# The weight tiles of a two-layer decoder kernel at the other end of SBUF

## The chip, the cores and the metric

The kernel runs on 1 core of one Trainium2 chip. The metric is the device time of one execution in microseconds (us), and the figure to be predicted is the median of several runs. Engines are named as the profile names them: PE (matrix multiplication), PEld (PE's weight loads), DVE, ACT, POOL, and SP, which only issues DMAs here.

## The reference

One sequence of 512 tokens with 1024 channels passes two layers. Four mixers (compressed and windowed attention, a diagonal state-space scan, a gated delta rule, a stick-breaking attention) work on slices of one large projection; their outputs are gated, projected and added, and a SwiGLU block follows.

```python
for l in range(DEPTH):                                   # 2
    h = rms_norm(x, attn_norm[l])
    proj = h @ w_in[l]                                   # 1024 x 6804
    (nsa_q, nsa_kv, nsa_g, s5_u, gdn_qkv, gdn_a, gdn_b, gdn_z, sb_qkv,
     merge_logits) = jnp.split(proj, IN_OFFSETS, axis=-1)
    o_nsa, o_s5, o_gdn, o_sb = ...                       # each (1, 512, 256)
    gates = jax.nn.sigmoid(merge_logits).reshape(B_, S_, N_BRANCH, D_MODEL)
    merged = jnp.zeros_like(x)
    for m, o_m in enumerate((o_nsa, o_s5, o_gdn, o_sb)):
        merged = merged + gates[:, :, m] * (o_m @ w_branch[l, m])
    x = x + merged @ w_out[l]
    x = x + swiglu_ffn(rms_norm(x, ffn_norm[l]), w_gate[l], w_up[l], w_down[l])   # 1024 -> 2816 -> 1024
```

## The kernel before, in words

Activations lie with the channels on the 128 partitions and the 512 tokens along the row. The weights stream through in slabs of 128 columns (512 KB, 4096 bytes a partition), 140 in each of the two layers, in one order that is written out by hand (`NAMES`). A slab passes three stations. SP's queue loads it into one of two places of `raw` (L426 and L430). ACT copies it into one of three places of `wH` with rounding to float32r (L1013). The rest, `raw - wH`, goes into `wL`, by POOL up to the first slabs of the branch projection (L1878) and by DVE from there on (L1331); that instruction also hands the place of `raw` back to SP.

Every large product is then made of three float32r matmuls, in the helper `mm3`: `wH x high`, `wH x low`, `wL x high`, where high and low are the two parts of the activation. They stand on L464, L465 and L466 of the kernel. The weights are the stationary operand (128 x 128, loaded by a LDWEIGHTS ahead of each matmul) and the activation is the moving operand (128 x 512). Which tiles move depends on the stage:

- the input projection, spread as `fill` between the small steps of the mixers, and the gate and up projections of the SwiGLU: `hH` and `hL`
- the branch projections: `oH` and `oL`, both in `arena`
- the output projection: `mH` and `mLow`, both in `pj`
- the down projection: `hidH` in `arena` and `hidL` from `pj` onward
- one pair of slabs a layer (`values`, "sbv") has the roles exchanged: `hH` and `hL` are loaded as weights and `wH` and `wL` move, 256 columns at a time.

SBUF is laid out by hand. The helper `sb` gives each tile the next free byte of the row, rounded up to 32 bytes, in the order of the calls; a tile with `at=` lies over another. Nothing else in the program depends on where a tile is.

Of the kernel before, what the change touches and what calls it, by code (L numbers as in the profile page):

```python
# [21 lines left out]
F32R = mybir.dt.float32r  # L22

P = 128
D = 1024
KT = D // P
# [73 lines left out]
RING = 2  # L100
SPLIT = 3
# [55 lines left out]
def program(nc, a_x, a_pos, a_const, a_pack, a_w, a_gates, a_out):  # L157
    with ExitStack() as ctx:
# [13 lines left out]
        def sb(name, shape, dt=F32, at=None, skip=0):  # L172

            size = int(np.prod(shape[1:])) * (2 if dt == BF16 else 4)
            if at is None:
                place[name] = top[0] = -(-top[0] // 32) * 32
                top[0] += size
            else:
                place[name] = place[at] + skip
            return nc.alloc_sbuf_tensor_at(name, shape, dt, offset=place[name])  # L180
# [4 lines left out]
        hH = sb("hH", [P, KT, S], F32R)  # L185
        hL = sb("hL", [P, KT, S], F32R)
        gload = sb("gload", [P, 4, 4, S], at="hH")
        raw = sb("raw", [P, RING, KT, P])
        wH = sb("wH", [P, SPLIT, KT, P], F32R)
        wL = sb("wL", [P, SPLIT, KT, P], F32R)  # L190
        cosT = sb("cosT", [P, S])
        sinT = sb("sinT", [P, S])
        small = sb("small", [P, 632])
# [9 lines left out]
        pj = sb("pj", [P, NPJ, S])  # L203
        sbv = sb("sbv", [P, NT, 256])
        gst = sb("gst", [P, 2, S])
        oH = sb("oH", [P, 8, S], F32R, at="arena")
        oL = sb("oL", [P, 8, S], F32R, at="arena", skip=4 * 4096)
        mH = sb("mH", [P, KT, S], F32R, at="pj")
# [1919 lines left out]
```

## Time and profile before

| | us |
|---|---|
| median of 3 runs | 2216.49 (2214.96 to 2217.32) |
| the profiled execution | 2215.63 |
| span of its instructions | 2213.8 |
| PE busy | 2059.3, 93% |
| DVE busy | 1196.2, 54% |
| ACT busy | 759.8, 34% |
| POOL busy | 540.4, 24% |

Busy means that an instruction of the engine was under way. PE's matmuls overlap in the records, so a busy PE says that it did not stand still, and not how fast it went; how fast is read from the distance of one matmul's start to the next one's.

### The profile page before, as it was taken

What the parts mean: (1) busy time and instruction counts of PE and PEld (TensorE: products, weight loads), DVE (VectorE), ACT (ScalarE), POOL (GpSimd) and SP (SyncE); (2) the same over time, 40 slices, a digit from 0 to 9 for tenths busy, and PEclk for the clock granted to TensorE, in tenths of its full rate; (3) what the DMA queues carried; (4) which work ended last, traced back from release to release, by engine and by line L of the source; (5) the groups of instructions that cost most, each with busy time, mean ns of one, the idle gap of its engine ahead of it and who ended that gap; (6) DMA issues with size and microseconds to landing.
All of it is one profiled execution on the core that took longest, in us unless ns stands there. A gap on an engine that the chain in (4) does not pass through costs nothing. (4 is left out here: it accounts for less than half of the span.)

```text
span 2213.8 us, 25834 instructions
## 1 busy us (share of the span) xinstructions
PE 2059.3 (93%) x10096; PEld 1651.2 (75%) x10096; DVE 1196.2 (54%) x1657; ACT 759.8 (34%) x1149; POOL 540.4 (24%) x304
## 2 busy tenths in 40 slices
PE   5998988899999999999979989889999999999998
PEld 3778977667777888888747879666577778888886
DVE  6635569764447555542266264796633575555421
ACT  5442231264335422222154422313642343322221
POOL 2435028523116000000034340484131240000000
PEclk9999989999989999999989999999999899999999
DMA  5221011222134233223242210113121442222332
GB/s 216 91 91 49 15 53 58 90 68 72 58 114 171 85 99 101 96 95 105 67 171 86 77 48 20 55 65 100 58 72 48 149 141 91 100 95 95 105 97 94
DMA packets 55124, 196.98 MB, mean 89 GB/s; under 512 B 6112, under 2 KB 6112, under 8 KB 52576
## 3 DMA queue, kind: packets, MB, share of 16 engines
q1 hardware_dynamic: 41184, 153.41, 21.1%
q10 hardware_dynamic: 13824, 41.95, 4.9%
q8 instruction: 82, 1.34, 0.3%
q14 instruction: 34, 0.28, 0.0%
HBM read 176.46 MB, written 18.87 MB: 88 GB/s over the span
## 5 line engine op out<-in xcount | busy, mean ns | idle before, releaser
L464 PE MATMUL bank<-hH,wH 128*128 128x512 f32 (+1 forms) x1536 | 617.5, 402 | 30.4 <-POOL wL L1878 14.9
L465 PE MATMUL bank<-hL,wH 128*128 128x512 f32 (+1 forms) x1536 | 605.7, 394 | 0.0
L466 PE MATMUL bank<-hH,wL 128*128 128x512 f32 (+1 forms) x1536 | 605.3, 394 | 0.0
L1878 POOL TENSOR_TENSOR wL<-raw,wH 128x1024 fp32r<-128x1024 f32 x114 | 282.2, 2480 | 1156.8 <-ACT wH L1013 1156.6
L1013 ACT ACTIVATE wH<-raw 128x1024 fp32r<-128x1024 f32 x276 | 289.6, 1051 | 295.8 <-PE bank L466 234.8
L464 PEld LDWEIGHTS bank<-hH,wH 128*128 128x128 f32 (+1 forms) x1536 | 291.9, 190 | 109.7 <-issue 30.1
L1331 DVE TENSOR_TENSOR wL<-raw,wH 128x1024 fp32r<-128x1024 f32 x162 | 214.2, 1322 | 253.0 <-ACT wH L1013 253.0
L466 PEld LDWEIGHTS bank<-hH,wL 128*128 128x128 f32 (+1 forms) x1536 | 291.0, 189 | 65.0 <-issue 1.1
L465 PEld LDWEIGHTS bank<-hL,wH 128*128 128x128 f32 (+1 forms) x1536 | 291.5, 190 | 62.1 <-issue 2.1
L1016 ACT ACTIVATE gst<-bank 128x512 f32<-128x512 f32 x64 | 38.2, 597 | 351.3 <-PE bank L466 351.3
L466 PE MATMUL bank<-hidH,wL 128*128 128x512 f32 x352 | 140.4, 399 | 0.0
L465 PE MATMUL bank<-hidL,wH 128*128 128x512 f32 x352 | 138.7, 394 | 0.0
L464 PE MATMUL bank<-hidH,wH 128*128 128x512 f32 x352 | 138.0, 392 | 0.0
L1647 DVE TENSOR_TENSOR arena<-arena 128x512 f32<-128x512 f32 x64 | 104.9, 1697 | 0.5
L1308 ACT ACTIVATE hidH<-arena 128x512 fp32r<-128x512 f32 x44 | 27.8, 633 | 191.3 <-DVE arena L1855 191.3
L1967 POOL TENSOR_TENSOR arena<-arena 128x512 f32<-128x512 f32 x48 | 80.8, 1685 | 25.3 <-DVE arena L1815 21.4
L1773 DVE TENSOR_REDUCE small<-bank 128x1 f32<-128x128 f32 (+3 forms) x64 | 30.8, 490 | 103.2 <-PE bank L876 101.8
L465 PEld LDWEIGHTS bank<-hidL,wH 128*128 128x128 f32 x352 | 66.1, 188 | 17.3
L464 PEld LDWEIGHTS bank<-hidH,wH 128*128 128x128 f32 x352 | 66.1, 188 | 15.7
L466 PEld LDWEIGHTS bank<-hidH,wL 128*128 128x128 f32 x352 | 66.1, 188 | 15.1
L1305 ACT ACTIVATE comp<-comp 128x512 f32<-128x512 f32 x44 | 27.8, 632 | 127.7 <-DVE comp L1846 127.7
L1642 DVE TENSOR_TENSOR_SCAN arena<-small,arena 128x512 f32<-128x512 f32 x32 | 58.1, 1855 | 0.5 <-POOL arena L1935 0.5
(394 smaller groups left out, 2988.0 us busy)
## 6 DMA issues: line engine op xcount, KB each, us to landing
raw<-weights SPq DMA_DIRECT2D x280, 512.0 KB, 3.5
gates<-gst ACTq DMA_DIRECT2D x64, 256.0 KB, 2.4
gload<-gates ACTq DMA_DIRECT2D x16, 1024.0 KB, 7.5
arena<-weights ACTq DMA_DIRECT2D x10, 512.0 KB, 9.0
xT<-x SPq DMA_DIRECT2D x1, 2048.0 KB, 9.8
pj<-weights ACTq DMA_DIRECT2D x4, 512.0 KB, 4.0
out<-xT SPq DMA_DIRECT2D x1, 2048.0 KB, 6.3
const<-constants SPq DMA_DIRECT2D x1, 1180.5 KB, 5.2
```

The source lines that it names most:

```text
L464: mm(out, a[0], b[0], start=start, stop=False)
L465: mm(out, a[0], b[1], start=False, stop=False)
L466: return mm(out, a[1], b[0], start=False, stop=stop)
L1013: act(wH[:, ORD[i] % SPLIT], raw[:, i % RING], ACT.Copy).then_inc(q["w_high"], 1)
L1016: act(out, stream(name)[:, :], ACT.Copy, scale=scale).then_inc(q["proj_taken"], 1)
L1305: act(ft[:, f % 2, :], fa[:, f % 2, :], ACT.Tanh, scale=0.5).then_inc(q["fg_tanh"], 1)
L1331: tt_(wL[:, ORD[i] % SPLIT], raw[:, i % RING], wH[:, ORD[i] % SPLIT].bitcast(F32), SU)\
L1642: v.tensor_tensor_scan(s5_z(i, j), mg, s5_m(i, 2 * j), 0.0, M, A_).then_inc(q["z_ready"], 1)
L1647: tt_(chunks(s5_m(i, j)), x, z, M).then_inc(q["n_ready"], 1)
L1773: v.tensor_reduce(nm[:, 4 * m + h:4 * m + h + 1], PS[2 + h % 2][:, 0:P * (m // 2 + 1)], AX_X, ALU.max, negate=True).then_inc(q["nm_ready"], 1)
L1878: tt_(wL[:, ORD[i] % SPLIT], raw[:, i % RING], wH[:, ORD[i] % SPLIT].bitcast(F32), SU)\
L1967: ins = tt_(mtmp[:, dt % 2, 0, :], mtmp[:, dt % 2, 0, :], mtmp[:, dt % 2, m, :], A_)
```

## The change: the place of three tiles

The three tiles `raw`, `wH` and `wL` (32,768 bytes a partition together) are given out last and no longer after `gload`. All that came behind them moves down by 32,768 bytes.

```diff
         hH = sb("hH", [P, KT, S], F32R)
         hL = sb("hL", [P, KT, S], F32R)
         gload = sb("gload", [P, 4, 4, S], at="hH")
-        raw = sb("raw", [P, RING, KT, P])
-        wH = sb("wH", [P, SPLIT, KT, P], F32R)
-        wL = sb("wL", [P, SPLIT, KT, P], F32R)
         cosT = sb("cosT", [P, S])
         sinT = sb("sinT", [P, S])
         small = sb("small", [P, 632])
...
         pj = sb("pj", [P, NPJ, S])
         sbv = sb("sbv", [P, NT, 256])
         gst = sb("gst", [P, 2, S])
+        raw = sb("raw", [P, RING, KT, P])
+        wH = sb("wH", [P, SPLIT, KT, P], F32R)
+        wL = sb("wL", [P, SPLIT, KT, P], F32R)
         oH = sb("oH", [P, 8, S], F32R, at="arena")
         oL = sb("oL", [P, 8, S], F32R, at="arena", skip=4 * 4096)
```

No instruction is added, removed or reordered on any engine, and no wait differs: the two programs are the same row by row but for the addresses in their operands. These are the starts that `sb` gives out, in bytes of a partition's row counted from the start of the first tile, `const`, which itself begins at a multiple of 128 (byte 16,512):

| tile | start before | remainder by 128, by 512 | start after | remainder by 128, by 512 |
|---|---|---|---|---|
| `hH` | 29,472 | 32, 288 | 29,472 | 32, 288 |
| `hL` | 45,856 | 32, 288 | 45,856 | 32, 288 |
| `raw` | 62,240 | 32, 288 | 179,584 | 0, 384 |
| `wH` | 70,432 | 32, 288 | 187,776 | 0, 384 |
| `wL` | 82,720 | 32, 288 | 200,064 | 0, 384 |
| `arena` (`oH`, `oL`, `hidH`) | 109,952 | 0, 384 | 77,184 | 0, 384 |
| `pj` (`mH`, `mLow`, `hidL`) | 167,296 | 0, 384 | 134,528 | 0, 384 |
| `gst` | 208,256 | 0, 384 | 175,488 | 0, 384 |

A place of a slab is 4096 bytes long and one k-step of a moving tile 2048, so the remainders hold for each of their pieces.

## Rows read from the trace of the kernel before

**Rows 1.** The page's head: busy us of each engine, share of the span, instructions.

```profile
PE 2059.3 (93%) x10096; PEld 1651.2 (75%) x10096; DVE 1196.2 (54%) x1657; ACT 759.8 (34%) x1149; POOL 540.4 (24%) x304
```

**Rows 2.** Stretches of layer 1: length, busy of PE, PEld, DVE, ACT, POOL, clock, DMA.

```profile
45.00:650.00 605.00, 554.94 (x3017) 444.21 (x3017) 346.87 (x510) 215.58 (x378) 221.88 (x123) 0.95 0.19 65
742.00:982.00 240.00, 240.00 (x1058) 198.33 (x1057) 128.95 (x156) 74.13 (x93) 0.00 (x0) 1.00 0.29 95
982.00:1110.00 128.00, 123.70 (x531) 99.18 (x529) 33.93 (x33) 23.82 (x23) 0.00 (x0) 1.00 0.27 87
```

**Rows 3.** PE's groups by shape, and one of its loads: count, busy us, mean ns, idle before.

```profile
L464 PE MATMUL bank<-hH,wH 128*128 128x512 f32 x1520 | 610.3, 401 | 20.4 <-POOL wL L1878 14.9 <-ACT arena L1085 5.5
L464 PE MATMUL bank<-hidH,wH 128*128 128x512 f32 x352 | 138.0, 392 | 0.0
L464 PE MATMUL bank<-oH,wH 128*128 128x512 f32 x128 | 52.3, 408 | 0.0
L464 PE MATMUL bank<-mH,wH 128*128 128x512 f32 x128 | 50.9, 398 | 2.7 <-DVE mLow L1335 2.7
L464 PE MATMUL bank<-wH,hH 128*128 128x256 f32 x64 | 18.9, 295 | 0.0
L464 PEld LDWEIGHTS bank<-hH,wH 128*128 128x128 f32 (+1 forms) x1536 | 291.9, 190 | 109.7 <-issue 30.1
```

**Rows 4.** Timeline of PE in the gate and up projections: start us, duration us.

```profile
900.04 0.39 PE L464 MATMUL bank<-hH,wH 128*128 128x512 f32 x1
...
902.08 0.39 PE L464 MATMUL bank<-hH,wH 128*128 128x512 f32 x1
```

**Rows 5.** The same in the down projection and, behind it, the output projection.

```profile
1029.94 0.39 PE L464 MATMUL bank<-hidH,wH 128*128 128x512 f32 x1
1030.17 0.39 PE L465 MATMUL bank<-hidL,wH 128*128 128x512 f32 x1
1030.40 0.40 PE L466 MATMUL bank<-hidH,wL 128*128 128x512 f32 x1
...
1032.04 0.39 PE L464 MATMUL bank<-hidH,wH 128*128 128x512 f32 x1
...
735.01 0.39 PE L464 MATMUL bank<-mH,wH 128*128 128x512 f32 x1
737.11 0.39 PE L464 MATMUL bank<-mH,wH 128*128 128x512 f32 x1
```

**Rows 6.** PE alone in three stretches: gate and up, down, branch projections.

```profile
755.00:980.00 225.00, 225.00 (x994) 1.00 0.31 99
985.00:1095.00 110.00, 110.00 (x473) 1.00 0.30 96
655.00:695.00 40.00, 40.00 (x173) 1.00 0.68 254
```

**Rows 7.** Timeline of PE where a projection slab starts after other work.

```profile
98.90 0.39 PE L465 MATMUL bank<-hL,wH 128*128 128x512 f32 x1
...
100.51 0.39 PE L466 MATMUL bank<-hH,wL 128*128 128x512 f32 x1
...
101.42 0.39 PE L464 MATMUL bank<-hH,wH 128*128 128x512 f32 x1
```

**Rows 8.** One line's instructions, ns min/median/max: ACT's rounding, DVE's and POOL's remainder.

```profile
L1013 ACT ACTIVATE wH<-raw x276: 1040/1049/1065, 19.0 to 2189.5; 128x1024 fp32r<-128x1024 f32 x138
L1331 DVE TENSOR_TENSOR wL<-raw,wH x162: 1224/1227/2324, 659.3 to 2190.6; 128x1024 fp32r<-128x1024 f32 x162
```

**Rows 9.** DMA issues: count, KB each, median us from issue to landing.

```profile
raw<-weights SPq DMA_DIRECT2D x280, 512.0 KB, 3.5
pj<-weights ACTq DMA_DIRECT2D x4, 512.0 KB, 4.0
```

**Rows 10.** Who waited for whom: us in total, times, longest us.

```profile
ACT wH L1013 <- DMA raw<-weights: 60.9, 27, 8.4
PE bank L464 <- POOL wL L1878: 14.9, 6, 5.5
```

## The prediction

> **What bounds the kernel now.** I read the page's head first: PE is busy 93% of the span of 2213.8 us, DVE 54%, the others less [rows 1]. Then the stretches of layer 1: while the mixers run, PE is busy 555 of 605 us, in the gate and up projections 240.00 of 240, in the down projection 124 of 128, and the granted clock is 0.95 to 1.00 of 2.4 GHz [rows 2]. So PE sets the time, and since the change touches no instruction, only two things can move it: how long an operation on a tile takes, or when a transfer into one lands. Both must be read as a dependence on the place of a tile.
>
> The groups of PE say what is at stake [rows 3]. With 128 loaded columns and 512 moving ones there are 3 x 1520 matmuls on `hH`/`hL`, 3 x 352 on `hidH`/`hidL`, 3 x 128 on `oH`/`oL` and 3 x 128 on `mH`/`mLow`, plus 3 x 64 with 256 columns in which the weight tiles themselves move. Of the 4560 on `hH`/`hL`, 2 x 44 x 24 = 2112 stand in the gate and up projections.
>
> Their distance from start to start is where a place shows. In the gate and up projections nine distances take 902.08 - 900.04 = 2.04 us, 226.7 ns each [rows 4]. In the down projection nine take 1032.04 - 1029.94 = 2.10 us, 233.3 ns, and in the output projection 737.11 - 735.01 = 2.10 us again [rows 5]. Long stretches agree: with the matmuls cut by the edges counted in, 225 us with 994 give 226.4 ns, 110 us with 473 in the down projection 232.6, and 40 us with 173 in the branch projections 231.2 [rows 6]. Same shape, same clock of 1.00, same instruction: the 6.6 ns hang on which tile moves. The distances also differ in form: on `hH` they are even, on `hidH` and `hidL` they run 0.23, 0.23, 0.24 us, three times in these 2.10 [rows 5]. And a slab on `hH` that starts after other work is slow first: seven distances of 230 ns (98.90 to 100.51), then 227 to 228 (100.51 to 101.42) [rows 7]. So the fast form is one into which the stream settles on some tiles and never on others.
>
> **What the change does to this, part by part.** `hH` and `hL` stay. `arena` and `pj` go down by 32,768 bytes and keep their remainders by 128 and by 512. The weight tiles go up by 117,344 bytes, and their remainder by 128 changes from 32 to 0. Three readings of the 6.6 ns are open.
>
> (a) The moving tile decides: by its start's remainder (32 for the pair at 226.7 ns, 0 for the three at 233.3), or by lying low in the row (226.7 ns up to byte 62,240, 233.3 from 109,952). By the remainder, no matmul on 512 columns changes. By the height, `oH`, `oL` and `hidH` would start at 77,184, between the two known sides, while `pj`, at 134,528, stays among those known at 233.3. If the step lay just below 109,952, some 384 matmuls on `oH`/`oL` and 16 of 22 pieces of the 704 on `hidH` would become fast, 896 x 6.6 ns = -5.9 us; with a step halfway, at 86,100, four pieces of 16 and four of 22, -1.5 us. The matmuls in which the weight tiles move get a slow mover: 192 x 6.6 ns = +1.3 us. Sum by the remainder +1.3, with the height 0 or less: I take +1, bounds -5 and +2.
>
> (b) The weights and the moving tile must agree. Before, the quicker pair has the weights' remainders (32 and 288) and the tiles at 233.3 have not. After, it is the other way round: weights, `arena` and `pj` agree at 0 and 384, and `hH` and `hL` are left alone. Then 1824 matmuls gain 6.6 ns, -12.0 us; the gate and up projections lose 2112 x 6.6 = +13.9 us, all on the path [rows 2]; the other 2448 on `hH` are slow for a third of each slab already [rows 7], which leaves 1632 x 6.6 = 10.8 us, of which PE's idle time between the mixers' steps (605 - 555 = 50 us in layer 1 [rows 2]) may swallow half, +5.4; and +1.3 from the weights that move. Sum +8.6, between +3 (all swallowed) and +14 (none).
>
> (c) The weights' own start matters, so that all distances change. No row has weights with another remainder, so this has no price of its own; from 233.3 and 226.7 ns the nearest bounds are 6.6 ns on the matmuls of one kind, either way.
>
> Between (a) and (b) no row decides. For (b) speaks that the slow pattern repeats every three matmuls, as the three loads do. For (a) speaks that a load takes 190 ns [rows 3] and is issued a matmul ahead, so it has 36 ns to spare even at the fast distance and need not meet anything in time. I give (a) somewhat more.
>
> **The other edits** cost nothing that I can find. ACT's rounding takes 1040 to 1065 ns over all three places of `wH` and both of `raw`, and DVE's remainder has a minimum of 1224 and a median of 1227 [rows 8], so engines off PE show no dependence on a place; what lengthens DVE to 2324 is not a place, as all three are used in turn. A transfer into `raw` (remainder 32) lands in 3.5 us, one into `pj` (remainder 0, issued amid others) in 4.0 [rows 9]. If a load took 0.5 us more or less, ACT would feel it in the 27 waits in which a load came last, and PE only in the six where it waits for POOL's remainder [rows 10]: 6 x 0.5 = 3 us either way. I take 0, since the 4.0 were measured in a queue.
>
> The Trainium skill, SBUF — State Buffer, section "Who interferes with whom", says that PE has two read ports of its own, one for the moving operand and one for weight loads, and never waits for anyone. By it neither the place of the weights nor that of the moving tile could matter, and the sum would be 0. The trace disagrees on the moving tile: 226.7 against 233.3 ns on the same ports [rows 4, 5].
>
> **The sum.** By (a) the profiled execution of 2215.63 us would become about 2217; against the median of 2216.49, 0.9 us higher, I forecast 2217.5 us: no change. Within 0.2%, 4.4 us, is about what a measurement of this kernel cannot tell from none.
>
> **The rivals.**
> 1. Agreement decides and `hH` loses, reading (b): 2216.5 + 8.6 = 2225, up to 2230. For it: every row at 226.7 has equal remainders. It decides as soon as the losses on `hH` pass 4.4 + 12.0 - 1.3 = 15.1 us, over 2112 + 816 matmuls 5.2 ns each, that is from a distance of about 232 ns. Price of its neighbour, in which `hH` slows and the other tiles stay slow: +13.9 + 5.4 to 10.8 + 1.3 = +21 to +26, 2237 to 2243.
> 2. Agreement helps `arena` and `pj`, and `hH` still settles with the new weights, since its own remainder stays: -12.0 + 1.3 = -10.7, 2206. For it: settling takes only some seven matmuls on `hH` [rows 7], so the stream may find a stable form at another offset. Against it: it needs the slow form to come from the weights alone, and one offset is as new as the other.
> 3. The height decides and all of `arena` that can comes below the step: -5.9 + 1.3, 2212. It is the lower end of (a).
>
> **How the numbers follow.** Reading (a) has 0.43 and is the likeliest: 2217.5, its own range 2212 to 2220. Rival 1 has 0.22, its neighbour 0.10, rival 2 with a gain by the weights' own start 0.25. So: faster by over 0.2% 0.25, within 0.43, slower 0.32. The range reaches down to rival 2 with its bound, 2203, and up over rival 1 into the neighbour, 2240; what is left out, the neighbour's upper half and larger gains from (c), is under 2 in 10.
>
> **What would show it.** By (a), nine distances in the gate and up projections again take 2.04 us and in the down projection 2.10. By rival 1 they trade places: 2.10 and 2.04, and the 240 us of the gate and up projections become 247. By rival 2 both read 2.04. ACT's 1049 and DVE's 1227 ns stay in all. I am wrong if the distances change at all in a stage with 512 moving columns, or if the waits for `raw` grow past 60.9 us and reach PE.

## The result, and the profile after

The changed kernel takes **2231.02 us** (median of 5 runs, 2225.48 to 2234.01) against 2216.49 before: a ratio of 1.0061, 95% interval 1.0045 to 1.0076. It became slower by 0.45 to 0.76%, more than the 0.2% that a measurement can tell from no change. The likeliest case of the prediction, no change by reading (a), did not happen; its first rival, reading (b), did. The profiled execution took 2225.48 us, the shortest of the five, with a span of 2223.7, 9.9 us above the span of before.

First PE alone in the gate and up, the down and the branch projections; the columns are the stretch, its length, PE's busy time (instructions), the granted clock, the DMA share and GB/s.

```profile
755.00:980.00 225.00, 225.00 (x960) 1.00 0.29 94
995.00:1095.00 100.00, 100.00 (x443) 1.00 0.33 106
655.00:693.00 38.00, 38.00 (x170) 1.00 0.75 281
```

At the same clock of 1.00, PE begins 960 matmuls in the 225 us of the gate and up projections instead of 994 [rows 6], 234.4 ns each. In the down projection 443 in 100 us are 225.7 ns, where 473 in 110 us gave 232.6, and in the branch projections 170 in 38 us are 223.5 where 173 in 40 us gave 231.2 (in all of them matmuls cut by the edges are counted in, so the true distances are up to 3 ns longer). The timeline shows the same in single steps, on `hH` and then on `hidH`:

```profile
899.93 0.40 PE L464 MATMUL bank<-hH,wH 128*128 128x512 f32 x1
...
902.04 0.40 PE L464 MATMUL bank<-hH,wH 128*128 128x512 f32 x1
...
1030.13 0.39 PE L464 MATMUL bank<-hidH,wH 128*128 128x512 f32 x1
...
1032.17 0.39 PE L464 MATMUL bank<-hidH,wH 128*128 128x512 f32 x1
```

Nine distances take 2.11 us on `hH` and 2.04 us on `hidH`, where they took 2.04 and 2.10 [rows 4, 5]. The two have traded places. PE's group on `mH` and one of its loads (count | busy us, mean ns | idle before), then what fills the weight tiles (ACT's rounding and DVE's remainder, ns min/median/max; the transfer, us from issue to landing):

```profile
L464 PE MATMUL bank<-mH,wH 128*128 128x512 f32 x128 | 51.4, 402 | 5.5 <-DVE mLow L1335 5.5
L464 PEld LDWEIGHTS bank<-hH,wH 128*128 128x128 f32 (+1 forms) x1536 | 292.0, 190 | 117.5 <-issue 29.2
L1013 ACT ACTIVATE wH<-raw x276: 1039/1048/1066, 19.0 to 2199.8; 128x1024 fp32r<-128x1024 f32 x138
L1331 DVE TENSOR_TENSOR wL<-raw,wH x162: 1224/1225/2321, 660.6 to 2200.9; 128x1024 fp32r<-128x1024 f32 x162
raw<-weights SPq DMA_DIRECT2D x280, 512.0 KB, 3.5
```

A recorded load lasts 190 ns as before [rows 3], the two engines take what they took [rows 8], and a transfer into `raw` 3.5 us [rows 9]. So neither the loads by themselves nor the feed of the weights changed, only how closely the matmuls follow each other.

Where the 9.9 us of the two profiles lie is read from the first and the last start of the first matmul of each three in a stage (count : ns min/median/max, first to last start in us). The first six rows are the kernel before, layer 1 and 2, then the changed kernel.

```profile
L464 PE MATMUL bank<-oH,wH x64: 399/399/764, 649.6 to 694.9; 128*128 128x512 f32 x64
L464 PE MATMUL bank<-mH,wH x64: 392/392/503, 695.6 to 741.3; 128*128 128x512 f32 x64
L464 PE MATMUL bank<-hidH,wH x176: 392/392/397, 982.3 to 1104.8; 128*128 128x512 f32 x176
L464 PE MATMUL bank<-oH,wH x64: 399/399/763, 1748.7 to 1794.0; 128*128 128x512 f32 x64
L464 PE MATMUL bank<-mH,wH x64: 399/399/502, 1794.7 to 1840.4; 128*128 128x512 f32 x64
L464 PE MATMUL bank<-hidH,wH x176: 392/392/397, 2081.4 to 2203.9; 128*128 128x512 f32 x176
```

```profile
L464 PE MATMUL bank<-oH,wH x64: 389/389/767, 650.8 to 695.0; 128*128 128x512 f32 x64
L464 PE MATMUL bank<-mH,wH x64: 389/389/628, 695.7 to 743.1; 128*128 128x512 f32 x64
L464 PE MATMUL bank<-hidH,wH x176: 387/389/393, 992.0 to 1111.0; 128*128 128x512 f32 x176
L464 PE MATMUL bank<-oH,wH x64: 389/389/767, 1753.3 to 1797.5; 128*128 128x512 f32 x64
L464 PE MATMUL bank<-mH,wH x64: 389/389/628, 1798.2 to 1845.8; 128*128 128x512 f32 x64
L464 PE MATMUL bank<-hidH,wH x176: 387/389/393, 2094.8 to 2213.8; 128*128 128x512 f32 x176
```

| stage, both layers together | how it is read | us |
|---|---|---|
| gate and up | last start on `mH` to first on `hidH`: 241.0 twice, then 248.9 and 249.0 | +15.9 |
| output projection | first to last start on `mH`: 45.7 twice, then 47.4 and 47.6 | +3.6 |
| down projection | first to last start on `hidH`: 122.5 twice, then 119.0 twice | -7.0 |
| branch projections | first start on `oH` to first on `mH`: 46.0 twice, then 44.9 twice | -2.2 |
| fillers and the rest | layer 1 up to `oH` +1.2; last start on `hidH` to first on `oH` 643.9, then 642.3 | -0.4 |

The sum is +9.9. The output projection is the odd line: its tiles agree with the weights now and yet it takes longer. The timeline and the clock show why:

```profile
700.20 0.39 PE L466 MATMUL bank<-mH,wL 128*128 128x512 f32 x1
703.21 0.50 PE L464 MATMUL bank<-mH,wH 128*128 128x512 f32 x1 [2.63 <-DVE mLow L1335]
...
706.01 0.63 PE L464 MATMUL bank<-mH,wH 128*128 128x512 f32 x1
706.44 0.63 PE L465 MATMUL bank<-mLow,wH 128*128 128x512 f32 x1
```

PE gets there sooner and waits 2.63 us for the last `mLow`, 5.5 us in both layers together (before, 2.7 [rows 3]). Some 1.5 us after the wait the matmuls begin to follow at 0.43 us. The granted clock says why, first of the stretch behind the wait in the changed kernel, then of the one in the kernel before:

```profile
703.50:707.00 3.50, 3.50 (x12) 0.67 0.05 19
```

```profile
702.50:706.50 4.00, 4.00 (x19) 1.00 0.02 6
```

Of its two levels, 1.2 and 2.4 GHz, the clock fell to the lower one for part of that time; before, it stayed at the upper. Over both layers the longer wait is +2.8 us and the nine longer distances behind each wait are +3.2 us; the shorter distances everywhere else give back 2.4 us, and that makes the +3.6.

### The profile page after: what moved, and what is told of

The parts are those of the page before. It is cut to its first block and busy times, and to the rows that moved or that the text cites. A ratio compares the mean times of both kernels' runs of the same rounds, so it can differ in the third digit from the quotient of the medians.

```text
span 2223.7 us, 25834 instructions
## 1 busy us (share of the span) xinstructions
PE 2073.6 (93%) x10096; PEld 1651.3 (74%) x10096; DVE 1202.0 (54%) x1657; ACT 759.8 (34%) x1149; POOL 539.1 (24%) x304
## 5 line engine op out<-in xcount | busy, mean ns | idle before, releaser
L464 PE MATMUL bank<-hH,wH 128*128 128x512 f32 (+1 forms) x1536 | 625.3, 407 | 30.1 <-POOL wL L1878 15.0
L465 PE MATMUL bank<-hL,wH 128*128 128x512 f32 (+1 forms) x1536 | 614.0, 400 | 0.0
L466 PE MATMUL bank<-hH,wL 128*128 128x512 f32 (+1 forms) x1536 | 613.6, 399 | 0.0
L464 PEld LDWEIGHTS bank<-hH,wH 128*128 128x128 f32 (+1 forms) x1536 | 292.0, 190 | 117.5 <-issue 29.2
L464 PE MATMUL bank<-hidH,wH 128*128 128x512 f32 x352 | 136.9, 389 | 0.0
L464 PEld LDWEIGHTS bank<-hidH,wH 128*128 128x128 f32 x352 | 66.1, 188 | 13.9
L1851 DVE TENSOR_TENSOR crot<-bank,crot 128x512 f32<-128x512 f32 x44 | 30.4, 690 | 56.1 <-PE bank L466 56.1
```

Source lines behind the costliest of these rows:

```text
L464: mm(out, a[0], b[0], start=start, stop=False)
L465: mm(out, a[0], b[1], start=False, stop=False)
L466: return mm(out, a[1], b[0], start=False, stop=stop)
L1851: tt_(fb[:, f % 2, :], PS[2 * ((f + 1) % 4) + 1][:, :], rs2, M).then_inc(q["ga_ready"], 1)
```

## The experiments

"Agree" means below that weights and moving tile start at the same byte modulo 256. Before, the weights and `hH`, `hL` do, and `arena` and `pj` are 96 bytes off; after the change it is the other way round (remainders by 512 in the table above). All experiments but e10 give the helper `sb` a number of free bytes ahead of a tile:

```diff
-        def sb(name, shape, dt=F32, at=None, skip=0):
+        def sb(name, shape, dt=F32, at=None, skip=0, pad=0):
...
-                place[name] = top[0] = -(-top[0] // 32) * 32
+                place[name] = top[0] = -(-top[0] // 32) * 32 + pad
```

| kernel | edit | median us (runs) | ratio to before, 95% interval |
|---|---|---|---|
| e1_top_equal | weights at the top, agreeing with `hH` again | 2216.31 (11) | 0.9998, 0.9988 to 1.0008 |
| e2_low_shifted | weights in their old place, 96 bytes up | 2227.60 (5) | 1.0049, 1.0036 to 1.0062 |
| e3_all_equal | old order, all agree | 2205.30 (6) | 0.9954, 0.9942 to 0.9966 |
| e4_three_offsets | slots 64, 128, 256 bytes off `hH` | 2228.10 (1) | |
| e5_low_part_off | all agree but `wL` | 2236.55 (4) | 1.0100, 1.0085 to 1.0115 |
| e6_small_offsets | slots 16, 32, 192 bytes off `hH` | 2221.23 (1) | |
| e7_warm_wait | e3 with 14 more matmuls a layer | 2207.74 (6) | 0.9965, 0.9952 to 0.9979 |
| e8_equal_again | e3 | 2203.39 (5) | 0.9945, 0.9932 to 0.9959 |
| e9_warm_again | e7 | 2207.80 (5) | 0.9963, 0.9949 to 0.9976 |
| e10_after_again | the changed kernel | 2230.64 (1) | |
| e11_top_all_equal | weights at the top, all agree | 2204.66 (5) | 0.9953, 0.9939 to 0.9966 |

**Place or remainder.** e1 is the changed kernel with 416 bytes ahead of `raw`:

```diff
-        raw = sb("raw", [P, RING, KT, P])
+        raw = sb("raw", [P, RING, KT, P], pad=416)
```

> The weights stay at the top of SBUF, as in the changed kernel, but 416 bytes higher, so that raw, wH and wL have the remainder of hH and hL (divided by 512) again and differ from hid, o and m, as before the change. If agreement of remainders sets the distance of the matmuls (reading b): hH and hL settle at 226.7 ns, hid, o and m at 233.3 ns, gate/up takes 228 us of a layer instead of 236, and the time is that of the kernel before, 2216.5 us, 0.6% under the changed kernel. If the place in SBUF sets it (the distance between weights and moving tiles, or which of them lies higher): it stays as after the change, hH and hL near 234 ns, hid, o and m at 226.7 ns, about 2226 to 2231 us.

e2 is the kernel before with 96 bytes ahead of `raw` (and 160 ahead of `cosT`, so that the tiles behind move by 256):

> The order of tiles of the kernel before, with 96 bytes of room ahead of raw and 160 ahead of cosT, so that raw, wH and wL are 96 bytes off hH and hL and a multiple of 256 bytes away from hid, o and m. If agreement of remainders sets the distance, and modulo 256 or less: the pattern of the changed kernel without its move, hH and hL at 234 ns, hid, o and m at 226.7 ns, 2226 to 2231 us. If it needs agreement modulo 512: hH and hL at 234 ns, hid, o and m still at 233.3 ns, about 7 us more than that, 2233 to 2238 us. If the place sets it: as before the change, 2216.5 us.

PE in the stretches of the gate and up and the down projection, e1 and then e2:

```profile
755.00:980.00 225.00, 225.00 (x992) 1.00 0.30 97
995.00:1095.00 100.00, 100.00 (x431) 1.00 0.29 96
```

```profile
755.00:980.00 225.00, 225.00 (x962) 1.00 0.29 94
995.00:1095.00 100.00, 100.00 (x443) 1.00 0.32 106
```

416 bytes bring back the pattern and the time of the kernel before with the weights still at the top, and 96 bytes make the pattern of the changed kernel without the move. Within the 0.1% of e1's interval the place counts for nothing; the low part of the addresses is what counts. e2 also shows that agreement modulo 256 is enough, since there the starts of `hidH` and of the weights differ by 256 modulo 512, and `hidH` still begins 443 matmuls in 100 us.

**All agree.** e3 is the kernel before with two edits, e11 the changed kernel with the same two:

```diff
-        hH = sb("hH", [P, KT, S], F32R)
+        hH = sb("hH", [P, KT, S], F32R, pad=96)
...
-        cosT = sb("cosT", [P, S])
+        cosT = sb("cosT", [P, S], pad=160)
```

> The order of tiles of the kernel before, with 96 bytes of room ahead of hH and 160 ahead of cosT, so that hH, hL, raw, wH and wL have one remainder (0 of 512) and hid, o and m the same modulo 256. If agreement modulo 256 or less sets the distance: all of them settle at 226.7 ns, 1824 matmuls save 6.6 ns each against the kernel before, which is 12 us: about 2204.5 us, 0.5% faster than before. If it needs agreement modulo 512, or if the place sets it: as before, 2216.5 us, with hH and hL at 226.7 ns and hid, o and m at 233.3 ns.

> The changed kernel, weights at the top, with 96 bytes of room ahead of hH and 160 ahead of cosT, so that all operands agree modulo 256. If the remainders are all there is to the change: every distance settles at 226.7 ns and the time is that of the other layout in which all agree, 2205 us, 1.1% below the changed kernel. If the place at the top costs anything of its own: more than 2209 us.

e3 and, behind it, e11 in the two stretches:

```profile
755.00:980.00 225.00, 225.00 (x994) 1.00 0.30 99
995.00:1095.00 100.00, 100.00 (x443) 1.00 0.30 95
```

```profile
755.00:980.00 225.00, 225.00 (x995) 1.00 0.30 97
995.00:1095.00 100.00, 100.00 (x443) 1.00 0.29 94
```

Both stages are at the short distance at once, and both kernels beat the one before by 0.3 to 0.6%. So what the changed kernel lost was not the price of the move: with 96 and 160 free bytes the same move gives 2204.66 us.

**How far off is off.** e4 puts the high and the low part of each weight slot side by side in one tile, `wpair`, and the three slots at three distances from agreement:

```diff
-        wH = sb("wH", [P, SPLIT, KT, P], F32R)
-        wL = sb("wL", [P, SPLIT, KT, P], F32R)
+        W_AT = [0, 2064, 4144]
+        wpair = sb("wpair", [P, 6 * KT * P + 48], F32R, pad=64)
...
+            at = W_AT[ORD[i] % SPLIT]
+            return wpair[:, at:at + KT * P].rearrange("p (k c) -> p k c", k=KT)
```

> The order of the kernel before, but the three weight slots, high and low part of each side by side, lie 64, 128 and 256 bytes off the remainder of hH and hL, and hid, o and m are 32, -32 and 96 bytes (modulo 256) off these slots. Successive weight slabs go through the slots in turn, so the timeline of one gate/up stage shows the three offsets one behind the other. If agreement modulo 64 is enough: all hH and hL slabs settle at 226.7 ns, hid, o and m slabs stay at 233 to 234 ns. Modulo 128: those of 64 bytes take 234 ns, the two others 226.7 ns. Modulo 256: only those of 256 bytes take 226.7 ns. Modulo 512: none. The time lies between 2216 us (all settle) and 2231 us (none does).

The starts of the last four slabs of the gate and up projections, `fg20` to `fu21`, in the slots at 256, 64, 128 and 256 bytes (a slab is 24 matmuls; L472 is L464 of the other kernels):

```profile
965.74 0.39 PE L472 MATMUL bank<-hH,wpair 128*128 128x512 f32 x1
...
971.17 0.40 PE L472 MATMUL bank<-hH,wpair 128*128 128x512 f32 x1
...
976.77 0.39 PE L472 MATMUL bank<-hH,wpair 128*128 128x512 f32 x1
...
982.35 0.39 PE L472 MATMUL bank<-hH,wpair 128*128 128x512 f32 x1
```

The first three slabs last 5.43, 5.60 and 5.58 us, that is 226, 233 and 232 ns a matmul, and the other slabs of the stage repeat this in turn. Only the slot at 256 bytes settles: 64 and 128 do not agree.

e6 is e4 with other offsets (`W_AT = [4, 2056, 4144]`, no free bytes ahead of `wpair` and 64 ahead of `cosT`, so that the tiles behind stay where e4 has them).

> The three weight slots lie 16, 32 and 192 bytes off the remainder of hH and hL, modulo 256. If only full agreement modulo 256 lets the matmuls settle: none of the gate/up slabs settles at 226.7 ns, all lie between 231 and 235 ns. If being near is enough (the same 64 bytes): the slots of 16 and 32 bytes settle at 226.7 ns and that of 192 does not. If only the distance around the circle of 256 counts: 192 shows what 64 showed, 233.4 ns.

The slab `fg13` in the slot at 16 bytes, first in layer 1 and then in layer 2 (from its start to the next slab's):

```profile
888.22 0.39 PE L472 MATMUL bank<-hH,wpair 128*128 128x512 f32 x1
...
893.67 0.39 PE L472 MATMUL bank<-hH,wpair 128*128 128x512 f32 x1
...
1988.58 0.39 PE L472 MATMUL bank<-hH,wpair 128*128 128x512 f32 x1
...
1994.18 0.39 PE L472 MATMUL bank<-hH,wpair 128*128 128x512 f32 x1
```

The starts of the last four slabs of layer 1, `fg20` to `fu21`, in the slots at 192, 16, 32 and 192:

```profile
965.73 0.40 PE L472 MATMUL bank<-hH,wpair 128*128 128x512 f32 x1
...
971.23 0.39 PE L472 MATMUL bank<-hH,wpair 128*128 128x512 f32 x1
...
976.83 0.39 PE L472 MATMUL bank<-hH,wpair 128*128 128x512 f32 x1
...
982.42 0.39 PE L472 MATMUL bank<-hH,wpair 128*128 128x512 f32 x1
```

192 bytes give 5.50 us (229 ns) and 32 give 5.59 (233 ns). In the slot at 16, `fu20` takes 5.60 us and `fg13` 5.45 (227 ns); from 780 us on, the slabs of layer 1 take the two values in turn, the `fg` slabs the short one and the `fu` slabs the long one. In layer 2 it is the other way round: `fg13` takes 5.60 us there and `fu20` 5.45, with the same tiles and the same PSUM bank. No theory had said that: near agreement is not enough, but the same slab in the same place can settle or not, so what ran before it must have a say. Nor does the distance on the circle of 256 bytes decide: 192 here and 64 in e4 are equally far from agreement, on opposite sides, and give 229 and 233 ns. The down projection of e6 shows that the side counts, with another moving tile: `hidH` lies 80 bytes above, 64 above and 96 below the three slots, and its slabs take 230, 229 and 234 ns a matmul.

**One part off.** e5 is e3 with 96 of its free bytes moved ahead of `wL`:

```diff
-        wL = sb("wL", [P, SPLIT, KT, P], F32R)
-        cosT = sb("cosT", [P, S], pad=160)
+        wL = sb("wL", [P, SPLIT, KT, P], F32R, pad=96)
+        cosT = sb("cosT", [P, S], pad=64)
```

> The layout in which all operands agree modulo 256, with one thing changed: 96 bytes of room ahead of wL, so that only the low parts of the weights are off. Of three matmuls in a row (wH with hH, wH with hL, wL with hH) only the third then has an operand that disagrees. If a matmul is longer because its own weights and its own moving tile disagree: the distance from the third to the next first one grows to some 233 ns, the other two stay at 226.7 ns. If it is the load of the next weights that meets the reads of the current moving tile: the second one's distance grows, since wL is loaded while hL streams. Either way about 6.6 ns on a third of 5900 matmuls, 13 us at most on the 2205.3 us of the layout that agrees, less what PE's idle time takes up: 2212 to 2218 us. If one operand that disagrees keeps the whole sequence from settling: all three near 233 ns and 2226 to 2233 us.

```profile
879.92 0.40 PE L466 MATMUL bank<-hH,wL 128*128 128x512 f32 x1
880.16 0.40 PE L464 MATMUL bank<-hH,wH 128*128 128x512 f32 x1
880.39 0.40 PE L465 MATMUL bank<-hL,wH 128*128 128x512 f32 x1
880.63 0.40 PE L466 MATMUL bank<-hH,wL 128*128 128x512 f32 x1
...
882.25 0.40 PE L464 MATMUL bank<-hH,wH 128*128 128x512 f32 x1
```

From 880.16 to 882.25 nine distances take 2.09 us, 232 ns each. Over the stretch from 760 to 975 us the mean distance is 233.3 ns behind a matmul of `wH` with `hH`, 231.7 behind `wH` with `hL` and 232.8 behind `wL` with `hH`: all three are longer. The third theory holds: one weight tile that disagrees, used by one matmul in three, keeps all of them from settling. Whether it is the load meeting the reads of the tile before, or the matmul's own pair, this run does not tell apart. Nothing settles in e5, neither on `hH` nor on `hidH`, and its median is above the 2226 to 2233 us that I had given.

**The wait in the output projection.** With all agreeing, PE again comes early to the last `mLow`: in e3 it starts no matmul for 3.55 us in layer 1, and the clock granted behind it is 0.55. e7 puts matmuls in that wait:

```diff
+                            if dt == 0 and k == KT - 1:
+                                for _ in range(14):
+                                    mm(PS[1][:, :], w[0][:, 0], oH[:, 0, :], start=True, stop=True)
                             if dt == 0:
                                 pe.wait_ge(q["merged_ready"], k + 1)
```

> The layout in which all operands agree, and in the output projection 14 more matmuls, of operands at hand into a bank that is not in use yet, ahead of the first wait for the last low part of the merged sums: no result uses them. There PE waits 3.3 us longer than a distance, and the granted clock then falls for some 8 matmuls at 427 ns. If the time lost there beyond the wait is that clock: the matmuls behind the wait stay near 227 ns, 1.6 us a layer come back, and the time falls from 2205.3 us to about 2202 us, 0.15%. If the wait is the bound and the clock recovers in time that is hidden anyway, or if the added matmuls run past the end of the wait: 2205 us or more.

> The layout in which all operands agree, once more, so that the one with added matmuls can be set against it on one chip. 2205.3 us as the first time; the stage from the fillers to the branch projections, which lasted 619.8 us in layer 2 there and 622.0 us with the added matmuls, shows how much of the difference is scatter of that stage.

> The same with the 14 added matmuls. Its output projection took 46.7 us of layer 1 against 48.5 us without them. If those 1.8 us a layer are real and the rest was scatter between chips: 0.1 to 0.2% below the layout without them on the same chip, about 2202 us. If the added matmuls cost elsewhere what they give back: no difference, or slower.

PE behind that wait, in e3 (layer 1) and then in e9:

```profile
702.50:706.20 3.70, 3.70 (x11) 0.55 0.01 6
```

```profile
698.00:702.00 4.00, 4.00 (x19) 1.00 0.07 28
```

The clock stays at its upper level and the output projection takes 46.2 us from its first to its last start on `mH` in e9's layer 1, against 47.9 in e3's. But the time does not follow: 2207.8 us against 2203.4 for e8 on the same chip. Without the added matmuls the wait varies: e3's layer 2 takes 44.7 us and e11's layer 1 as well, without a fall of the clock, while the added matmuls make it 46.0 to 46.2 us in every layer; so what they save in one layer they cost in another. Where the 4.4 us between the two medians lie is not shown, since e9's profiled execution is its shortest (2203.53 us) and e8's is one of its longer ones (2206.33). The edit is no gain.

**The scatter.** e10 is the changed kernel once more.

> The changed kernel once more, for a second profile beside the one of 2225.5 us, since its runs lie between 2225 and 2234 us. If the distances that don't settle scatter by themselves: gate/up (248.3 us a layer from its first matmul to the first of the down projection) differs between the two. If it is the stage of the fillers: that one differs (622.1 us in layer 2), and gate/up and down stand as they were.

```profile
L464 PE MATMUL bank<-oH,wH x64: 389/389/628, 655.1 to 699.6; 128*128 128x512 f32 x64
L464 PE MATMUL bank<-mH,wH x64: 389/389/499, 700.3 to 746.1; 128*128 128x512 f32 x64
L464 PE MATMUL bank<-hidH,wH x176: 387/389/392, 995.0 to 1114.1; 128*128 128x512 f32 x176
```

Gate and up take 248.9 us again (995.0 less 746.1) and down 119.1. Of the 5.2 us between the two spans (2228.9 and 2223.7) the fillers give +4.3 in layer 1 and +2.3 in layer 2, and the output projection -1.9, most of it in layer 1, where the clock did not fall behind the wait (45.8 us instead of 47.4). So the stage of the fillers scatters, and with the clock the output projection; the gate and up and the down projections don't. This execution took 2230.64 us, about the median of the changed kernel, so the part of the +14.5 us that the first profile does not show lies, in this one at least, in the fillers.

## Why the prediction was wrong

The likeliest case was no change, at 2217.5 us, and the kernel became 14.5 us slower. The median lies inside the stated range of 2203 to 2240 us, but that range was drawn around (a), (b) and the rivals together, so it says nothing for (a), on which the forecast stood; and by the prediction's own sign, "if the distances change at all in a stage with 512 moving columns", it was wrong.

- **What bounds the kernel, and where a place shows:** right. The distance from start to start moved, and with it the wait for `mLow` and the clock behind it; DVE's remainder (median 1225 ns in the changed kernel, 1227 before), ACT's rounding (1048, 1049) and the transfer into `raw` stayed, as the price of 0 for the other effects had it.
- **The step that failed** is the choice between (a) and (b): "a load takes 190 ns and is issued a matmul ahead, so it has 36 ns to spare even at the fast distance and need not meet anything in time." The loads still take 190 ns in the record, and the distance on `hH` went from 226.7 to 234.4 ns all the same. So spare time of a load does not show that the place it reads from is of no account. The evidence on the other side was named and weighed less. Of its two parts, the equal remainders of the quicker pair were the sound one. The other, that the long form repeats every three matmuls as the three loads do, holds for the kernel before only: in the changed kernel the long form on `hH` repeats every seven (232, 237, 238, 231, 234, 235 and 233 ns).
- **Reading (a)** falls in both forms. By the moving tile's remainder, `hH` would have kept its distance; by its height, e1, which lies within 416 bytes of the changed kernel, would not have had the time of the kernel before.
- **Reading (c)**, the weights' own start, falls as well: in the changed kernel the weights have one start for all stages, and the distance on `hH` grew while that on `hidH` shrank.
- **Rival 1** had the mechanism and the place: "they trade places: 2.10 and 2.04, and the 240 us of the gate and up projections become 247". They became 2.11, 2.04 and 248. Its sum of +8.6 us stands beside +9.9 between the profiles and +14.5 between the medians, and 2231.02 us is 1 us above the upper end that it gave. By terms: gate and up +13.9, measured +15.9, since a moving tile 96 bytes below the weights costs 7.7 ns a matmul, and the 6.6 had been measured 96 bytes above; `hidH`, `hidL` -7.0 (1056 of the 1824) as predicted; `oH`, `oL` -2.5, measured -2.2; `mH`, `mLow` -2.5, measured +3.6, because PE comes sooner to a wait for DVE and the clock falls behind it, which the prediction had nowhere. The rest of `hH` with the weights that move, +5.4 and +1.3, is -0.4 in one profile and +6.2 in e10 (655.1 less 649.6 in layer 1; 1758.7 less 1114.1, against 643.9, in layer 2), so it is mostly within the scatter of that stage.
- **Its neighbour and rival 2** each need only one of the two stages to change, and both changed. e3 and e11 are what rival 2 forecast (2206), but only by letting `hH` agree too.
- The Trainium skill, SBUF — State Buffer, section "Who interferes with whom", has PE read the moving operand and the weights through two ports of its own and wait for nobody. No row here shows a wait between ports, but the sum of 0 that the prediction drew from it is not what was measured: the changed kernel and e11 differ in the starts of tiles alone, and by 1.2% (2231.02 against 2204.66 us).

What stays open: what in the chip makes agreement modulo 256 matter. The runs show the rule and not the part that collides; whether the load or the matmul's own pair is concerned could not be told, because one weight tile off takes all three matmuls along. How much an unsettled distance costs the fillers is not settled either: they end at 650.8 and 655.1 us in the changed kernel, and between 644.8 and 651.7 in the five profiles in which all operands agree.

## What to carry to other kernels

Where PE runs matmul behind matmul, read the distance of their starts for each pair of operands, not the recorded durations; two distances for one shape at one clock were the sign here that the tiles' starts differ in a way that matters. In an SBUF laid out by hand, let the starts of all weight tiles and all moving tiles agree modulo 256 bytes: 256 free bytes gave this kernel about 0.5% (shown for float32r with 512 moving columns, and for no other type or shape). A move of tiles should be tried with the remainders held, or it measures the remainders and not the move.

## What the runs showed of the hardware that was not expected

- With 128x128 float32r weights and 512 moving columns at the full clock, matmuls follow at 226.7 ns where all operands agree modulo 256 bytes. Off agreement most lie between 229 (moving tile 64 bytes above the weights, e6) and 234.4 ns (96 below, the changed kernel), with 230 at 80 above, 232 at 128 bytes and 233 at 32 and 64 below and 96 above.
- One weight tile off, used by one matmul in three, takes all three matmuls from the short distance (e5).
- With the moving tile 16 bytes below the weights, slabs take 227 and 233 ns in turn, and the same slab took one value in layer 1 and the other in layer 2 (e6): the state in which a slab starts has a say.
- Behind the wait for the last `mLow` the granted clock fell in some executions and not in others: it fell in e3 after 3.55 us between two starts (layer 1, granted clock 0.55 behind it) and in e6 after only 2.27 us (layer 1, 0.66), and stayed at 1.00 in e8 after 3.72 us (layer 1). What decides it is not seen in these runs.
